# Second block for tiles 0-1 and then tiles 2-3, with a new last stage in fp32r parts

## The reference, cut to what matters

```
act = gelu(einsum('td,thkd->thk', hc, ue))
x = x + einsum('thk,thkd->td', g * act, ve)
```

```
score = einsum('bqhs,bqh->bqs', relu(q_idx . k_idx), w)   # sparse: top 128 keys of each query
tail  = cumsum(log_rest, reverse) - log_rest               # stick: a = exp(log_sigmoid(z) + tail)
mix = concat([oA * silu(gA), oB * silu(gB)])
h = layer_norm(ALPHA * x + mix @ w_out)
```

## Time and profile before

| | us |
|---|---|
| median of three runs | 2978.68 (2978.52 to 2986.62) |
| profiled execution, its own time | 2977.82 |
| its span | 2976.1 |
| everything before the first step | 0 to 1602 |
| first step (tiles 0-1, rows of tile 2) | 1602 to 2156 |
| second step (tile 2, rows of tile 3) | 2156 to 2656 |
| third step (tile 3) | 2656 to 2976 |
| busy in the span: PE, DVE, ACT, POOL | 2409.9, 1745.8, 911.2, 982.1 |

### The profile page before, as it was taken

The page is one execution under the profiler, slowest core; times in us unless marked ns, Lnnn a source line. Parts: engine busy times, 40 slices in busy tenths (PEclk is TensorE's granted clock), DMA queues, the critical chain, the costliest instruction groups (busy, mean ns, idle before and its releaser), DMA issues. The chain is left out here.

```text
span 2976.1 us, 30377 instructions
## 1 busy us (share of the span) xinstructions
PE 2409.9 (81%) x9779; PEld 1614.1 (54%) x9779; DVE 1745.8 (59%) x3656; ACT 911.2 (31%) x1742; POOL 982.1 (33%) x691
## 2 busy tenths in 40 slices
PE   6997999869878888898786996798557467549897
PEld 4776878758663334343333654575345345437574
DVE  3444311032136988988875678587759869865151
ACT  4444222233322222222212433143234314323232
POOL 2332555343232244344342234224323532420001
PEclk9998999989989999999898997899768778769898
DMA  4321333223139899999999899899799999965553
GB/s 158 98 67 50 96 98 102 79 83 124 52 125 343 313 407 413 415 412 397 395 414 404 325 370 356 343 365 393 303 358 373 416 406 377 386 268 196 216 190 140
DMA packets 257323, 805.56 MB, mean 271 GB/s; under 512 B 18366, under 2 KB 139862, under 8 KB 191655
## 3 DMA queue, kind: packets, MB, share of 16 engines
q0 software_dynamic: 73728, 536.90, 44.8%
q1 hardware_dynamic: 183463, 267.06, 25.6%
HBM read 795.07 MB, written 14.07 MB: 272 GB/s over the span
## 5 line engine op out<-in xcount | busy, mean ns | idle before, releaser
L1337 POOL DMA_INDIRECT gathered<-in_peer_rows,experts x436 | 530.4, 1216 | 923.5 <-DVE x_res L2630 616.3
L1695 PE MATMUL peer_banks<-gathered,peer_diags 128*128 128x512 f32 x720 | 338.3, 625 | 53.1 <-ACT peer_diags L1750 53.1
L78 PE MATMUL group_banks<-group_x_t,group_ring 128*128 128x128 f32 (+1 forms) x2016 | 342.9, 334 | 15.9 <-ACT group_x_t L2442 8.4
L78 PEld LDWEIGHTS group_banks<-group_x_t,group_ring 128*128 128x128 f32 x2016 | 310.1, 210 | 46.7 <-ACT group_x_t L2442 10.8
L2616 DVE CUSTOM_DVE_ANT_0 gathered<-gathered,late_nat 128x1024 f32<-128x1024 f32 x256 | 315.6, 1235 | 33.2 <-DMA gathered<-in_peer_rows,experts 28.1
L2630 DVE SCALAR_TENSOR_TENSOR x_res<-gathered,group_weights,x_res 128x1024 f32<-128x1024 f32 x256 | 328.3, 1283 | 2.7 <-DVE group_weights L2622 0.3
L1695 PEld LDWEIGHTS peer_banks<-gathered,peer_diags 128*128 128x128 f32 x720 | 142.5, 201 | 238.3 <-issue 238.3
L2256 PE MATMUL group_banks<-group_ring,group_x_t 128*128 128x512 f32 x512 | 235.7, 616 | 23.2 <-DMA group_ring<-in_weights 23.2
L1790 DVE CUSTOM_DVE_ANT_0 peer_product<-gathered,early_nat 128x1024 f32<-128x1024 f32 x180 | 214.7, 1223 | 37.8 <-DMA gathered<-in_peer_rows,experts 37.7
L1695 PE MATMUL peer_banks<-early_gathered,peer_diags 128*128 128x512 f32 x304 | 150.4, 647 | 53.4 <-ACT peer_diags L1750 53.4
L2256 PEld LDWEIGHTS group_banks<-group_ring,group_x_t 128*128 128x128 f32 x512 | 99.1, 198 | 146.5 <-issue 118.9
(11 more groups left out here) (376 smaller groups left out, 4211.8 us busy)
## 6 DMA issues: line engine op xcount, KB each, us to landing
group_ring<-in_weights SPq DMA_DIRECT2D x270, 512.0 KB, 6.1
mixer_wq<-in_w_in SPq DMA_DIRECT2D x24, 512.0 KB, 4.1
mixer_wk<-in_w_in SPq DMA_DIRECT2D x24, 512.0 KB, 4.1
peer_w<-in_w_pq SPq DMA_DIRECT2D x8, 1024.0 KB
gathered<-in_peer_rows,experts POOLq DMA_INDIRECT x436
diff_wv<-in_w_in SPq DMA_DIRECT2D x8, 512.0 KB, 4.1
conv_wb<-in_w_in SPq DMA_DIRECT2D x8, 512.0 KB, 4.1
merge_w<-in_w_conv_out SPq DMA_DIRECT2D x8, 512.0 KB, 3.5
```

The source lines that it names most:

```text
L78: last = nc.tensor.matmul(out, lhsT, rhs, start=n == 0, stop=n == len(pairs) - 1)
L1337: nc.gpsimd.indirect_dma_start(row_buffer(m, r), None, A["peer_rows"], bass.IndirectOffsetOnAxis(ap=at, axis=0))\
L1695: last = nc.tensor.matmul(ps[:, ACC[unit % 2] + half, :], diags[:, r % DIAGS, :], row_buffer(m, r)[:, D + half * BANK:D + (half + 1) * BAN ...
```

## The change

`GROUPS` becomes `((0, 1), (2, 3))`. `group_stage` is called once, for tiles 0-1, beside the 256 rows of tiles 2 and 3, and stores no output. A new `last_stage` then computes tiles 2 and 3 together. In it

- all products with weights, of the inputs `x_t` and `mix_t`, run as `three_passes` in fp32r; ACT writes the high part of each of the 90 blocks (`high_blocks`) and POOL the low part (`low_block`); blocks are loaded into a ring of four (`raw`) and split into a ring of six (`parts`);
- DVE writes the low parts of the inputs (`low_input`, `low_mix`);
- the attentions go by units of one tile and one pair of heads (16 a layer, a = 2 x pair + tile), with the same four steps per unit as before per pair, and one of the two head products, queries or keys, in front of each unit;
- bias tiles have three buffers, and the expert rows are done;
- the output of tiles 0 and 1 is written at the end, behind that of tiles 2 and 3.

```diff
-GROUPS = ((0, 1), (2,), (3,))
+GROUPS = ((0, 1), (2, 3))
...
-                sp.wait_ge(normed, 2 * NT * (LAYERS + 1))
-                for t in tiles:
-                    sp.dma_start(out[t * P:(t + 1) * P, :], m.x[:, t, :]).then_inc(stored, 16)
...
+    WS, PS, BS = 4, 6, 3
...
+                def load_block(n):
+                    if n >= WS:
+                        sp.wait_ge(w_split, n - WS + 1)
...
+                def load_affine(l):
+                    sp.wait_ge(normed, 2 * NT * (l + 1))
...
+                for t in range(first):
+                    sp.dma_start(out[t * P:(t + 1) * P, :], m.x[:, t, :]).then_inc(stored, 16)
...
+                def low_block(n):
+                    pool.wait_ge(w_high, n + 1)
+                    low_part(nc.gpsimd, parts[:, n % PS, LOW, :], raw[:, n % WS, :], parts[:, n % PS, HIGH, :]).then_inc(w_split, 1)
...
+                    for a in range(HALF_UNITS):
+                        heads(l, "qk"[a % 2], a // 2 + 1)
+                        tails(l, a)
+                        if a == 3:
+                            natural(l, "v", SPARSE)
+                        if a + 1 < HALF_UNITS:
+                            stick_logits(l, a + 1)
+                        else:
+                            sparse_logits(l, a + 1)
+                        stick_out(l, a)
...
+                def high_blocks(begun, upto):
+
+                    for n in range(begun, min(upto + PS + 1, LAYERS * BLOCKS)):
+                        act.wait_ge(w_loaded[n % WS], 16 * (n // WS + 1))
+                        if n >= PS:
+                            act.wait_ge(*block_used(n - PS))
+                        nc.scalar.activation(parts[:, n % PS, HIGH, :], raw[:, n % WS, :], ACT.Copy).then_inc(w_high, 1)
+                    return max(begun, min(upto + PS + 1, LAYERS * BLOCKS))
...
+                inverse_roots(0)
+                begun = high_blocks(0, -1)
...
+                    gates(l, STICK)
+                    begun = high_blocks(begun, block_at(l, STICK, "g", 3))
+                    for a in range(HALF_UNITS):
+                        u = a // 2 + 1
+                        (copy_keys if a % 2 else copy_queries)(l, u)
+                        stick_weights(l, a)
+                        begun = high_blocks(begun, block_at(l, u // PAIRS, "qk"[a % 2], u % PAIRS))
+                        if a == 3:
+                            copy_values(l, SPARSE)
+                            begun = high_blocks(begun, block_at(l, SPARSE, "v", 3))
+                        if a + 1 < HALF_UNITS:
+                            softplus(l, a + 1)
...
+                        if a == HALF_UNITS:
+                            gates(l, SPARSE)
+                            begun = high_blocks(begun, block_at(l, SPARSE, "g", 3))
...
-            for number in range(len(GROUPS) - 1):
-                group_stage(nc, A, m, number, out)
-        group_stage(nc, A, m, len(GROUPS) - 1, out)
+            group_stage(nc, A, m)
+        last_stage(nc, A, m, out)
```

More of the change, by code:

```diff
@@ L1951, in __init__, with group_stage @@
         self.at["end"] = self.steps
-def group_stage(nc, A, m, number, out):
-    ctx, sb, banks, sem = stage(nc, f"group{number}")
-    tiles = GROUPS[number]
-    first, last, NT = tiles[0], tiles[-1], len(tiles)
-    OLD = first * P
+def group_stage(nc, A, m):
+    ctx, sb, banks, sem = stage(nc, "group")
+    tiles, next_tiles = GROUPS
+    last, NT = tiles[-1], len(tiles)
     NQ = NT * P
-    keeps = number + 1 < len(GROUPS)
-    next_tiles = GROUPS[number + 1] if keeps else ()
     searched = [t for t in tiles if t >= 1]
@@ L1979, in group_stage @@
     job_at = {job: n for n, job in enumerate(jobs)}
-    O_BANK = {(half, t): 6 + (n if NT == 2 else half) for half in range(2) for n, t in enumerate(tiles)}
+    O_BANK = {(half, t): 6 + t for half in range(2) for t in tiles}
     def block_at(l, *name):
@@ L2604, in _ @@
                     done = gelus((l, "norm"), done)
-                gelus("end", done) if bg.rows else None
+                gelus("end", done)
             @block.vector
```

771 lines of the change are left out of this document (678 added, 93 removed).

## The result

| | before | after |
|---|---|---|
| median of the comparison, us (4 runs each) | 2982.65 | 3066.85 |
| lowest and highest | 2978.52, 2993.53 | 3060.96, 3072.47 |
| span of the profiled execution | 2976.1 | 3070.7 |

The kernel is slower: the ratio is 1.0276, 95% interval 1.0239 to 1.0314. The windows by step of the profile after; the columns are those of the earlier trace rows, and its three steps stand against the two here.

What follows compares the result with a forecast made beforehand. DMA was taken to bound the first step and mainly a serial chain the last stage: 1602 us unchanged + 830 + 621 = 3053 us of span, forecast 3055 us, 2.6% slower; range 2968 to 3110.

Steps and rivals of the forecast that it cites:

- three rivals: PE bounds the last stage (chance 0.14); both parts favourable, time even (0.08); first step fills DMA worse, 3119 us (0.12).
- First step: Step beside 256 rows: DMA queue time 805 us binds before DVE's 741; at a share of 0.97, 830 us.
- Last stage: Tiles 2 and 3 together: start, two layers, end give 606 us, plus 15 for contention, 621; bounds 573 and 669.
- index part: Layer's beginning in the last stage: index keys, head weights, four index queries, stick values and two free banks, 32.5 us.
- scores up to the first tails: Value copies, block copies, 16 scores, logits: 22.4 us; then stick gate's product, a head product, a bank wait: 15.
- loop: Stick loop of a layer, serial chain: units at 10.6 and 8.7 us, sparse values' product and ACT's late copies; 90 us.
- to the output: After the second turned weights: six more units, 39 us, then 7.5 us to the output.
- output and border: Layer's end: output 22.2 us, 3.5 for a falling clock, 15.6 for two tiles' sums, norms, transposes and low parts.
- The start: Last stage's bound to its first product: 31.5 us, with ACT's block copies before the input copies; contention up to 6.
- the end: Last stage's finish: 12.7 us without the next layer's transposes, then 9.5 from store to end.
- Contention: Last stage: DVE instructions with two SBUF inputs slowed beside POOL's low parts; 20 us if all meet, 15 taken.
- The rival of PE: PE's work bounds the last stage: 525 us, whole 2960, 0.6% faster; chance 0.14.

Runs made afterwards that it cites:

- e1: Changed kernel without the second half of the columns in the background's dot products and additions, all gathers kept; 3036.35 us, first step 815 us.
- e5: Changed kernel with GpSimd writing only 8 of 1024 columns of each weight block's low part in the last stage; 3034.68 us.
- e6: Changed kernel with ACT's copies of weight blocks in the stick loop moved behind the next softplus, two a unit at most; 3121.44 us.
- e8: Changed kernel with the next unit's stick logits ahead of this unit's tails, softplus ahead of stick weights, two suffix-sum buffers; 3085.6 us.
- e4: Changed kernel's last stage with float32 products from a ring of ten blocks, no high copies or low parts of weights; 3028.41 us.
- e12: Changed kernel with copies inside natural products, reordered start, earlier output of tiles 0-1, next logits before tails, head product and block copy moved; 2988.25 us.
- e3: Changed kernel with two of three passes of every product with weights left out in the last stage, copies, low parts and loads kept; 2978.56 us.

## Why the prediction was right, point by point

The forecast was 3055 us, 2.6% slower; measured are 3067 and 2.8%. The forecast's case held, and its three rivals did not come. The signs it named were there: DVE busy 716 us at a share of 0.95, a clock of 0.74, the first product 35 us behind the bound, the first layer 290.5 us long, waits in front of the second unit's tails (2.67 us) and the second turned weights (4.49), 90 low parts of 2.41 us. The bounds of its range are looser than its parts: the low end supposes a share of 1.01, where no first step here ran above 0.97, and the high end takes 650 for the last stage where its own bound was 669.

**First step: 830 predicted, 848 measured** (844.7 from first load to first load). The queue time was right (805 against 807 us), and DVE's work a little high (741 against 716). What was mis-sized is the share: 0.97 was taken, with the argument that DVE finds PE's results ready oftener; 0.95 came, near the 0.94 of the second step. e1 shows where the rest is: with a light DVE the share does reach 0.97, and the step 815 us, with 16 us less of queue time as well. The argument looked at DVE's waits for the layer, but DVE's own row work, at 0.84 of the time, is what leaves the queues gaps. The window's 381 GB/s, like the two rates before, stand above the 358 GB/s that the prediction set them against. The Trainium skill gives about 435 GB/s as the bound of one core that is alone (Perfetto Trace Analysis, Roofline). No run here exceeds that.

**Last stage: 621 predicted, 620.7 measured.** By pieces, in the table's terms: index part 32.5 predicted, 37.9 measured; scores up to the first tails 37.4 and up to 7 of contention, against 40.6; loop 90 against 90.0; 12 against 10.0; 24 against 21.7; to the output 46.5 against 51.1; output and border 41.3 against 39.2. The start was 31.5 and up to 6, measured 35 from the bound; the end 12.7 + 9.5 = 22.2, measured 20.0. Two errors of 5 us lie where I counted PE at full clock. In the index part the first product took 4.5 us instead of 2.95, the head weights 8.2 instead of 5.9 and the index queries 13.7 instead of 11.8, at granted clocks of 0.63 and 0.64 at first. In the part up to the output PE ran at 0.50 behind its wait for the second turned weights:

```profile
2685.34 1.97 PE L3142 MATMUL last_banks<-ident,last_near 128*128 128x128 f32 x8 [4.49 <-ACT last_near L3319]
...
2686.00:2700.00 14.00, 13.39 (x59) 11.61 (x58) 6.15 (x8) 4.36 (x8) 11.75 (x5) 0.50 0.62 211
```

Four other pieces (12, 24, the output and the end) came out about 2 us shorter each. That the sum meets 620.7 to within a microsecond is luck, two errors of 5 us one way against several of 2 the other way; that it lies near 620 is not.

**The loop: 90 predicted, 90.0 measured, by a mechanism that was half right.** I read one pair per 10.57 us as the latency of the chain. The same trace says that PE was hardly ever idle in it:

```profile
2733.20 1.12 PE L2304 MATMUL group_banks<-group_work,neg_tri 128*128 128x512 f32 x2 [0.19 <-DVE group_suffix L2699]
```

It waits 0.19 us of the 10.57, so chain and PE's work were about equally long already. In the last stage the two units of a pair were put at 10.6 and 8.7 us. Measured are 9.7 to 9.9 with a wait of 1.35 to 1.50, and 9.3 with none (from the tails at 2632.78 to those at 2642.07): the chain decides in front of tile 3's tails, PE in front of tile 2's. "There the cheaper product saves nothing" holds for half of the units only.

**Contention: 15 us taken, and 20 if all met.** The place was right (scaling of the input, score sums), and so was the size: in e5 the first product comes 3.9 us earlier and the scores of a layer are 5.0 us shorter, 13.9 together. The other 20 of e5's 34 us lie in the loops, the index part and the sparse half, where blocks are also loaded earlier; no run separates the two. But the prediction let the rule spare `soft` as a whole. That holds for its first instruction, which reads PSUM; the suffix sums behind it have both inputs in SBUF, and e6 and e8 show how exposed they are. The changed kernel spares nearly all of them by the place of one copy, which I had counted as pure cost on the chain.

**The rival of PE.** Its mechanism is half true: e4, the loop of e12, and half of the loop's units in the changed kernel itself are bound by PE. What kept the changed kernel from it was the order of ACT's copies and the start, as the forecast said. Its price of 525 us was not reached by any run that computes everything: e12 took 534.0 from its first load at 2456.6. The prediction let the rival decide from 541 us on with a first step of 830; with e12's stage beginning at 2456.6 that point lies at 2976.1 - 2456.6 = 519.5, and by its profile e12 is indeed still 14.5 us slower than the profile of before. By the medians of one occasion, where before had 2990.46 and not 2982.65, it is even.

**What stays open.** Whether a last stage under 534 us can be had with this grouping was not tried; PE's work of 473 us in e12, 13 us up to the first product and 17 behind the last leave some 31 us. How much of the 38 us between e4 and the changed kernel are the low parts and how much ACT's copies is known only roughly: e5 took 32 for the low parts, but it also brings the loads forward. What makes the clock fall behind one wait (2.67 us) and not behind another (2.86 us) of the same loop is not shown.

## What to carry to other kernels

When work hides transfers, count what is left uncovered: here two of three steps ran under the rows, and after the change only one did, so the rows' time fell by 206 us (554 + 500 to 848) while the uncovered time grew by 301 (320 to 621). An engine's copy that feeds GpSimd has two prices, its own time on its engine and the time of what GpSimd then meets on DVE; put it where DVE has no work with two SBUF inputs, and inside waits that exist anyway. A long gap on PE's chain can be paid twice, once as the gap and once as a slow stretch behind it, as at the second unit (2.67 us, then a clock of 0.50); behind the gaps of 1.35 us in the same loop the clock stayed at 1.00, so take the longest first.

## What the runs showed that I had not expected

- Less work made PE slower: in e3 PE's records in the loop fell from 533 to 388, its granted clock from 0.94 to 0.80, and the loop grew from 90.0 to 96.0 us.
- A suffix sum of 128 x 256 takes 0.43 us alone and 2.17 to 2.65 us beside a low part of GpSimd of 2.4 us: it takes as long as GpSimd's instruction does, nearly six times its own time, so short instructions lose most.
- The gain of moving copies into waits was larger than the copies: 12 copies of 1.05 us a layer, 12.6 us at most, gave a layer that is 20 us shorter (270.7 instead of 290.5), and at the same time the clock in the loop rose from 0.94 to 1.00 and the low parts left the score sums.
